# The first chunk of an mLSTM head's prompt state, computed in two pieces around the sixth state unit

## What is computed

```python
S = einsum('bhtd,bhsd->bhts', qc, kc) * exp(Dm - m_t)
num = inter * einsum('bhtk,bhkv->bhtv', qc, C) + einsum('bhts,bhsv->bhtv', S, vc)
kw = kc * w_s
C_new = scale * C + einsum('bhsk,bhsv->bhkv', kw, vc)
```

## Time and profile before

| | |
|---|---|
| three runs, median (lowest to highest) | 1884.65 us (1881.69 to 1885.49) |
| profiled execution | 1882.92 us |
| its span | 1881.2 us |
| PE busy / PE weight loads | 1842.8 us (98%) / 1726.9 us (92%) |
| DVE / ACT / POOL busy | 970.4 / 781.1 / 742.2 us |
| DMA, mean over the span | 112 GB/s |
| DMA in the slices that hold the heads | 235 to 310 GB/s |

### The profile page before, as it was taken

One profiled execution on the slowest core, in us unless ns is written; L12 is line 12 of the kernel. 1 busy time (PEld: TensorE's weight loads), 2 busy tenths in 40 slices (PEclk: granted clock), 3 DMA queues, 4 the chain that ended last, 5 costly groups with the idle time before them and its releaser, 6 DMA issues.

```text
span 1881.2 us, 33626 instructions
## 1 busy us (share of the span) xinstructions
PE 1842.8 (98%) x13546; PEld 1726.9 (92%) x13546; DVE 970.4 (52%) x1305; ACT 781.1 (42%) x1223; POOL 742.2 (39%) x622
## 2 busy tenths in 40 slices
PE   7999999999999999999999999999999999999997
PEld 7999999999999999998566665999999999999997
DVE  6787645524634522697776667322255336426313
ACT  4576835322322334443543444423454323323333
POOL 3333554352342344565232312554644433422541
PEclk9999999999999999999999999999999999999999
DMA  4222232322322322422389779322233222333221
GB/s 131 85 84 75 90 97 73 91 89 84 86 89 85 90 79 79 98 70 99 132 272 309 235 265 310 92 85 72 86 101 96 90 85 81 90 87 86 85 82 65
DMA packets 187435, 210.71 MB, mean 112 GB/s; under 512 B 24611, under 2 KB 150179, under 8 KB 187247
## 3 DMA queue, kind: packets, MB, share of 16 engines
q1 hardware_dynamic: 187074, 208.71, 36.1%
q10 hardware_dynamic: 224, 0.07, 0.0%
HBM read 168.09 MB, written 40.64 MB: 111 GB/s over the span
## 4 chain that ended last, share of the span: by engine, by line
PE 85%; DVE 5%; ACT 3%; DMA 2%; POOL 2%; issue 2%; SPq 0%; ACTq 0%; DVEq 0%; POOLq 0%
PE ps L2571 40%; PE ps L2714 23%; PE ps L2694 11%; DMA out_ml_C_s_dram<-C_HALVES 2%; PE ps L2955 2%; PE ps L3054 1%; PE ps L3016 1%; PE ps L2994 1%; PE ps L2889 1%; POOL W_LO L768 1%; DVE H_PAD L1903 1%; POOL K_LO L1005 1%; POOL V_LO L1013 1%; DVE C_HALVES L2376 1%; PE ps L3004 0%
## 5 line engine op out<-in xcount | busy, mean ns | idle before, releaser
L768 POOL TENSOR_TENSOR W_LO<-W_RAW,W_HI 128x512 fp32r<-128x512 f32 x392 | 545.2, 1402 | 555.5 <-ACT W_HI L1091 532.0
L1091 ACT ACTIVATE W_HI<-W_RAW 128x512 fp32r<-128x512 f32 x412 | 254.1, 628 | 500.7 <-PE ps L2571 257.5
L2571 PE MATMUL ps<-A_HI,W_HI 128*128 128x288 f32 x1144 | 247.5, 298 | 6.8 <-DVE A_LO L1739 4.8
L2571 PE MATMUL ps<-A_HI,W_LO 128*128 128x288 f32 x1144 | 245.7, 297 | 0.0
L2571 PE MATMUL ps<-A_LO,W_HI 128*128 128x288 f32 x1144 | 245.5, 297 | 0.0
L2571 PEld LDWEIGHTS ps<-A_HI,W_HI 128*128 128x128 f32 x1144 | 185.1, 190 | 9.3 <-issue 6.7
L2571 PEld LDWEIGHTS ps<-A_LO,W_HI 128*128 128x128 f32 x1144 | 185.3, 190 | 0.0
L2571 PEld LDWEIGHTS ps<-A_HI,W_LO 128*128 128x128 f32 x1144 | 185.2, 190 | 0.0
L871 POOL TENSOR_TENSOR G_LO<-GATED,G_HI 128x1152 fp32r<-128x1152 f32 x22 | 58.9, 2675 | 236.8 <-ACT G_HI L1335 236.6
L2714 PE MATMUL ps<-A_HI,W_HI 128*128 128x288 f32 x576 | 123.4, 296 | 0.0
L2714 PE MATMUL ps<-A_HI,W_LO 128*128 128x288 f32 x576 | 123.4, 296 | 0.0
(11 more groups left out here) (469 smaller groups left out, 4111.6 us busy)
## 6 DMA issues: line engine op xcount, KB each, us to landing
W_RAW<-in_ffn_w_up_dram SPq DMA_DIRECT2D x176, 256.0 KB, 2.8
C_HALVES<-in_state_mlstm_C_dram SPq DMA_DIRECT2D x64, 512.0 KB, 5.3
out_ml_C_s_dram<-C_HALVES SPq DMA_DIRECT2D x64, 512.0 KB, 5.4
W_RAW<-in_ffn_w_down_dram SPq DMA_DIRECT2D x88, 256.0 KB, 2.8
W_RAW<-in_ml_w_in_dram SPq DMA_DIRECT2D x64, 256.0 KB, 2.7
W_RAW<-in_rg_w_in_dram SPq DMA_DIRECT2D x48, 256.0 KB, 2.7
W_RAW<-in_ple_w_gate_dram SPq DMA_DIRECT2D x32, 256.0 KB, 2.8
W_RAW<-in_ml_w_out_dram SPq DMA_DIRECT2D x32, 256.0 KB, 2.9
```

Of the source, the lines that this page charges most:

```text
L768: pool.tensor_tensor(W_LO[:, s], W_RAW[:, s], W_HI[:, s].bitcast(F32), ALU.subtract).then_inc(lo_ready, 1)
L1091: act.activation(W_HI[:, s], W_RAW[:, s], ACT.Copy).then_inc(hi_ready, 1)
L2571: ins = pe.matmul(ps[:, 4 * s + 2 * m + h, 0:HALF_T], a[:, w, k, wc], x[:, h * HALF_T:h * HALF_T + HALF_T], start=i == 0 and k == 0 and q ...
```

## The change

PE: the passes of `cp0` are cut in two. The eight by the high parts of the values come behind unit 4, as before; the four by their low parts come behind unit 5 instead of ahead of it. The bank stays taken through unit 5. The table names the pieces in the order in which they end, so `cp0` now comes behind `u5`. SP: the stores of `cp0` and `cp1` move from steps 10 and 12 to steps 11 and 13, that of `cp0` behind `spread_rows`.

```diff
@@ head_order
-            ("u4", UNIT_BANKS), ("cp0", (3,)), ("u5", UNIT_BANKS), ("cp1", (1,)), ...
+            ("u4", UNIT_BANKS), ("u5", UNIT_BANKS), ("cp0", (3,)), ("cp1", (1,)), ...
@@ sync engine, loop over v
                     if v == 11 and h + 1 < HEADS:
                         spread_rows(h + 1)
-                    if v in (10, 12, 14):
-                        store_cp(h, v // 2 - 5)
+                    if v in (11, 13, 14):
+                        store_cp(h, {11: 0, 13: 1, 14: 2}[v])
@@ state_passes
+                    if part == 2 and kc == 0:
+                        pe.wait_ge(v_low, 4 * h + i + 1)
@@ prompt_state
-                if kc == 0:
-                    pe.wait_ge(v_high, h + 1)
-                    pe.wait_ge(k_high, 4 * h + 4)
-                take(h, f"cp{kc}")
+                if kc:
+                    take(h, f"cp{kc}")
                 for i in range(4):
-                    ins = state_passes(h, kc, i, bank, (0, 1, 2) if kc else (0,))
+                    ins = state_passes(h, kc, i, bank, (0, 1, 2) if kc else (2,))
...
+            def states_of_high_values(h):
+
+                bank = at(h, "cp0")
+                pe.wait_ge(v_high, h + 1)
+                pe.wait_ge(k_high, 4 * h + 4)
+                for part in range(2):
+                    if part:
+                        pe.wait_ge(k_low, h + 1)
                     for i in range(4):
-                        state_passes(h, 0, i, bank, (1,))
...
+                        state_passes(h, 0, i, bank, (part,))
@@ PE, loop over the heads
                 unit(h, 4)
+                take(h, "cp0")
+                states_of_high_values(h)
+                unit(h, 5)
                 prompt_state(h, 0)
-                unit(h, 5)
                 prompt_state(h, 1)
```

More of the change, by code:

```diff
@@ L115, in head_order @@
     tail = [("u2", UNIT_BANKS), ("ds", (1,)), ("pv2", (2,)), ("n0", (0,)), ("u3", UNIT_BANKS), ("pv3", (3,)), ("den", (2,)),
-            ("u4", UNIT_BANKS), ("cp0", (3,)), ("u5", UNIT_BANKS), ("cp1", (1,)), ("hp", (2,)), ("u6", UNIT_BANKS), ("cn", (3,))] \
+            ("u4", UNIT_BANKS), ("u5", UNIT_BANKS), ("cp0", (3,)), ("cp1", (1,)), ("hp", (2,)), ("u6", UNIT_BANKS), ("cn", (3,))] \
         + [("next qs", (2,)), ("next ks", (3,))] * (h + 1 < HEADS) \
@@ L3059, in prompt_state @@
                 bank = at(h, f"cp{kc}")
-                if kc == 0:
-                    pe.wait_ge(v_high, h + 1)
-                    pe.wait_ge(k_high, 4 * h + 4)
-                take(h, f"cp{kc}")
+                if kc:
+                    take(h, f"cp{kc}")
                 for i in range(4):
-                    ins = state_passes(h, kc, i, bank, (0, 1, 2) if kc else (0,))
+                    ins = state_passes(h, kc, i, bank, (0, 1, 2) if kc else (2,))
                     if between and i < 3:
                         between(i)
-                if kc == 0:
-                    pe.wait_ge(k_low, h + 1)
-                    for i in range(4):
-                        state_passes(h, 0, i, bank, (1,))
[L3072 to L3075, removed]
+                done(h, f"cp{kc}", ins)
+            def states_of_high_values(h):
[5 more added lines that the diff above has]
+                        pe.wait_ge(k_low, h + 1)
+                    for i in range(4):
+                        state_passes(h, 0, i, bank, (part,))
             def prompt_sums(h):
```

## The result

The change makes the kernel slower: 1919.75 us (median of four runs, 1916.65 to 1925.47) against 1885.07 us (1881.69 to 1887.89) for the kernel before on the same chip. The ratio is 1.0188, 95% interval 1.0158 to 1.0219, so +34.7 us by the medians. The forecast was slower, at 1903.5 us; the measured time lies above its range. So the two traces differ by 42.6 us, 8 us more than the medians, and sums from them come out larger than the medians allow.

The account below looks back on a forecast made before the run. PE, busy 1842.8 of 1881.2 us, was taken to bound the kernel. Waits +12.9 and clock +6.0 gave +18.9 on the profiled 1882.92, so 1901.8; with the median 1.7 above that execution, 1903.5 us, range 1893 to 1912.

Parts of the forecast that it names:

- the chain: Store of `cp0` issued later, landed, `cp2` copied, then `cp3`: PE idle some 5 us in heads 0 to 2.
- the rival with the fast landing: The store of `cp0` lands in 2.7 us instead of 5.9, clock left high: +3.0, 1887.7 us; chance 0.05.
- the waits' sum: PE's added waits for the late store of `cp0`, heads 0 to 3: 5.7 + 3.6 + 3.4 + 0.2 = +12.9 us.
- The store of `cp1`: Moved by one step, it gates the copy of `cp3`: 0, between 0 and +1 us a head.
- head 0's gain at unit 5: In head 0 PE waits 1.4 us for unit 5's second load, so the gain there was counted as 0.
- PE's own gain: Waits for V_LO hidden by unit 5: 3.0 us in heads 1 and 2, 0 in heads 0 and 3.
- the term for the clock: Work behind the long waits of heads 0 to 2 runs at half rate: 2.0 us a head, +6.0 us.
- The rival that I set against it: The waits come but the clock does not fall: +12.9, 1897.5 us; chance 0.17.

Follow-up runs that it names:

- the extra place: The change, late stores included, with `cp2` copied into SUMS, so its copy no longer waits for the store of `cp0`: 1880.94 us, ratio 0.9985.
- the second experiment: The kernel before with only the stores of `cp0` and `cp1` moved to steps 11 and 13, PE's order untouched: 1915.56 us, ratio 1.0159.
- the stores put back: The change with the stores of `cp0` and `cp1` back at steps 10 and 12, PE's split of `cp0` kept: 1882.6 us, ratio 0.9994.
- The two places with PE held up: The kernel before with PE paused in heads 0 to 2, ahead of unit 2 (1930.49 us) or, in a second kernel, ahead of `cp3` (1944.99 us).
- the products behind the wait: The change with 24 more products of 128 x 512 right behind PE's wait in heads 0, 1 and 2: 1921.94 us, ratio 1.0205.

## Why the prediction was right and where it was wrong

**Right: the direction and the chain.** Late issue, landing, copy of `cp2`, `cp3`. I expected waits of about 5 us in heads 0 to 2; they were 5.25, 5.72 and 4.96 us. The store of `cp0` took 6.9 us to land in head 1, and the 16 stores of the change 2.0 to 6.9, 5.5 in the middle, so the rival with the fast landing (0.05) falls. The price of the Trainium skill's page "DMA: Bandwidth & Descriptors" (the anatomy of one DMA), an estimated 2.6 us for this size, is given there for transfers that GpSimd issues. These are issued by SP; the last store of each head, with the DMA engines busy for 0.36 to 0.57 of the time, took 2.0 to 2.4 us, near that price, and the other twelve took 4.8 to 6.9 (while that of `cp0` was under way in heads 1 and 2, the share was 1.02 and 0.99). That ACT's wait is the link is shown by the extra place, which removes it with the stores left late; that the stores alone do it, by the second experiment.

**Right: the waits' sum.** Forecast +12.9 us, by head 5.7, 3.6, 3.4 and 0.2; it was 14.9 in the profiled execution, by head 6.1, 4.6, 3.6 and 0.5, where the landing in head 1 was 1 us longer than I took. The store of `cp1` cost nothing that the trace shows, and head 0's gain at unit 5 went into a wait for its load (1.85 us, 1.4 expected).

**Partly wrong: PE's own gain.** I put 3.0 us on heads 1 and 2 for the case that nothing comes behind, and 0 on heads 0 and 3. With the stores put back it was 1.8 in heads 1 and 2 and 1.0 in head 3, less 0.5 in head 0. At unit 5 it was 1.36 us in head 1 of the change (from unit 4's second half to the first pass of `cp1`, 6.33 to 4.97 us), near my 1.5. I had looked for the next load in head 0 and at unit 7 of head 3, not at unit 6 of the others.

**Wrong: the term for the clock.** This is the step that failed: "I take 2.0 us a head, between 0 and 3.4 (a whole stretch of 6.83 us at half rate)", +6.0 us. It measured 25.2 us in the profiled execution, 7 to 8 us in each of heads 0 to 2 and 3.3 in head 3, for which I had counted none. The reason I gave for the 2.0 was a wait of the same length at the start of the kernel. What stands behind that wait is a row of products of 128 x 288 and nothing else for 8 us. In `cp3` small products (64 x 64 and 128 x 32) stand among the passes, and behind it come those of the next head's beginning (32 x 512 and 128 x 128), and there the clock did not come back for 15.7 to 17.9 us of work in heads 0 to 2. The two places with PE held up show this difference in heads 1 and 2 (2 us against 7) but not in head 0, and the products behind the wait show it from the other side. That it is the small products that matter, and not some other difference of the two places, is argued from these runs.

The rival that I set against it argued with "a whole head of dense work" between the waits, which the trace would have refuted: in the stretch from `cp3` to the next unit 0 PE was busy for 20.70 of 21.02 us, but in 179 products, mostly narrow ones. That rival counts three stretches of low clock and the rows show two. The third stands at the beginning of head 0, behind a wait of 0.91 us:

```profile
909.51:916.34 6.83, 5.99 (x16) 4.04 (x14) 5.46 (x13) 2.77 (x5) 1.53 (x4) 0.50 0.11 39
```

There 5.99 us of work ran at half rate, small products first, with 0.84 us more of idle time in it. That is more than the 4.48 us behind the long wait that I took my price from, and a hint that the length of the wait is not what to go by. With 25.2 in place of 6.0 my sum is 1884.65 + 12.9 + 25.2 = 1922.8, against 1919.75 measured; part of the 3 us above belongs to the long profiled execution.

**Open.** Why the clock was not back ahead of the small products in head 0 with the hold ahead of unit 2, and what decides behind a wait of 1.0 to 1.3 us. Which of the narrow products keep the clock down was not tried one by one.

## What to carry to other kernels

When a piece of work is moved back, its store moves back too, and behind the store stands whoever needs the buffer next: follow the slot to its next writer before you count the gain. A wait on TensorE costs its length and then what the work behind it costs at half rate until the clock returns. Here a busy share did not tell how long that is; which products stand behind the wait told more. So take the price from a wait that stood ahead of the same kind of work.

## What the runs showed of the hardware

- In the change the granted clock stayed at 0.50 for 13.65 to 20.48 us at a time, with PE busy for 62.30 of 68.27 us, under passes of 128 x 512 with small products among them and then 32 x 512 and 128 x 128 ones. Under 24 products of 128 x 512 in a row it was back 2.83 and 5.05 us after the restart.
- The same small products ran at 1.00 in the kernel before, where no wait stood ahead of them: the granted clock was 1.00 from 1029.39 to 1050.41 us.
- Waits of 1.33 and 1.32 us at the same place of the program: one was followed by 13.65 us at half rate, the other by none. One of 2.18 us ahead of unit 5 in head 0 (the extra place) was followed by none.
- 100 increments of a semaphore by PE's own queue held it up for 11.6 to 14.0 us. The record of one is 51 ns long, which had made me expect 5.1, but in both traces the next one starts 151 ns behind it. In head 1 with the hold ahead of unit 2 they run from 1012.19 to 1027.53 us, while PE still has products to run for the first 4 us.
